# Latents, rotation and beta masks moved, delta level products without warming repeats, last MLA scores and values between output products: a four-layer fp32 transformer on one core

## The reference

```python
a_mat = beta[..., :, None] * jnp.einsum('nhcid,nhcjd->nhcij', k, k) * d_strict
sol = lax.linalg.triangular_solve(a_mat, rhs, left_side=True, lower=True, unit_diagonal=True)
```

## Time and profile before

| what | us |
|---|---|
| median of 3 runs | 1282.39 (1282.03 to 1291.31) |
| the profiled execution | 1290.47 |
| its span in the trace | 1288.3 |
| TensorE busy | 1237.2 |
| VectorE busy | 734.5 |
| ScalarE busy | 352.6 |

### The profile page before, as it was taken

The page is one execution under the profiler, slowest core; times in us unless marked ns, Lnnn a source line. Parts: engine busy times, 40 slices in busy tenths (PEclk is TensorE's granted clock), DMA queues, the critical chain, the costliest instruction groups (busy, mean ns, idle before and its releaser), DMA issues. The chain is left out here.

```text
span 1288.3 us, 18514 instructions
## 1 busy us (share of the span) xinstructions
PE 1237.2 (96%) x7285; PEld 885.2 (69%) x7285; DVE 734.5 (57%) x1467; ACT 352.6 (27%) x756; POOL 46.0 (4%) x92
## 2 busy tenths in 40 slices
PE   7999999999999999999999989999899999998997
PEld 5887548996446674599944468658567587575783
DVE  3154366766443135567644448883886178856872
ACT  2253311211002134112200043242551232425422
POOL 1100000000000000000000000100200000102000
PEclk9999899999999999999999999998999999999999
DMA  9732105545543532335445453130010433210000
GB/s 278 261 133 70 66 1 197 193 137 194 171 156 130 175 109 108 128 136 195 146 181 195 139 157 130 67 131 1 1 51 1 165 130 131 83 50 1 2 2 33
DMA packets 65854, 149.25 MB, mean 116 GB/s; under 512 B 2098, under 2 KB 8136, under 8 KB 65768
## 3 DMA queue, kind: packets, MB, share of 16 engines
q1 hardware_dynamic: 62432, 141.63, 31.3%
q0 software_dynamic: 1216, 3.52, 1.0%
q10 hardware_dynamic: 2119, 2.91, 0.9%
HBM read 146.95 MB, written 1.07 MB: 115 GB/s over the span
## 5 line engine op out<-in xcount | busy, mean ns | idle before, releaser
L1368 ACT ACTIVATE region<-banks 128x384 f32<-128x384 f32 (+8 forms) x159 | 77.1, 485 | 298.4 <-PE banks L444 104.9
L444 PE MATMUL banks<-hnT,weight_slabs 128*128 128x256 f32 x576 | 126.6, 380 | 3.4 <-DVE hnT L1856 3.4
L444 PEld LDWEIGHTS banks<-hnT,weight_slabs 128*128 128x128 f32 x576 | 108.8, 190 | 20.1 <-DVE hnT L1856 4.1
L496 PE MATMUL banks<-weight_slabs,region 128*128 128x512 f32 x256 | 115.1, 592 | 0.0
L496 PEld LDWEIGHTS banks<-weight_slabs,region 128*128 128x128 f32 x256 | 48.5, 190 | 60.3 <-issue 60.3
L496 PE MATMUL banks<-region 128*128 128x512 f32 x192 | 87.6, 592 | 0.0
L1839 DVE TENSOR_TENSOR region<-weight_slabs 128x1024 f32<-128x1024 f32 x32 | 39.2, 1225 | 80.3 <-PE banks L496 76.4
L1839 DVE TENSOR_TENSOR region<-region 128x256 f32<-128x256 f32 (+23 forms) x160 | 74.2, 464 | 16.9 <-ACT region L1725 11.8
L1997 DVE TENSOR_TENSOR region<-banks,region 128x128 f32<-128x128 f32 x40 | 11.7, 292 | 120.4 <-PE banks L611 95.3
L1839 DVE TENSOR_TENSOR region<-weight_slabs,region 128x1024 f32<-128x1024 f32 x64 | 78.2, 1221 | 1.1
L496 PEld LDWEIGHTS banks<-region 128*128 128x128 f32 x192 | 36.5, 190 | 45.9 <-issue 45.9
(11 more groups left out here) (364 smaller groups left out, 2045.6 us busy)
## 6 DMA issues: line engine op xcount, KB each, us to landing
weight_slabs<-in_mlp_w SPq DMA_DIRECT2D x32, 2048.0 KB, 8.9
weight_slabs<-in_w_in SPq DMA_DIRECT2D x10, 2048.0 KB, 7.8
weight_slabs<-in_od_w_in SPq DMA_DIRECT2D x6, 2048.0 KB, 8.0
weight_slabs<-in_ev_w_in SPq DMA_DIRECT2D x4, 2048.0 KB, 10.6
weight_slabs<-in_w_out SPq DMA_DIRECT2D x4, 2048.0 KB, 8.9
weight_slabs<-in_ev_w_out SPq DMA_DIRECT2D x2, 2048.0 KB, 8.0
weight_slabs<-in_od_w_out SPq DMA_DIRECT2D x2, 2048.0 KB, 7.7
weight_slabs<-in_w_in SPq DMA_DIRECT2D x2, 2016.0 KB, 7.7
```

The costliest lines, as they stand in the source:

```text
L444: ins = mm(view(ps, b + i * S, (1, S)), view(slabs, o + k * width + c0, (1, P)), view(hnT, k * S, (1, S)), start=k == 0, stop=k == KC - 1)
L496: ins = mm(view(ps, b, (1, 512)), view(R, act + k * st, (1, P)), view(w, wt + k * step_, (1, 512)), start=n == 0 and k == 0, stop=n == 7 a ...
L1368: say(A(dst, view(ps, b, *(dims or ((1, n),)), np_=np_), ACT.Copy, scale=scale), read("scalar", *key))
```

## The change

- TensorE: the `cT` transposes move into the RWKV inverse, behind its last Z products (hook "X"). Decay groups 2 and 3 come behind the `Yr` products of the second chunk instead of ahead of them.
- Seven of the eight warming products of the delta inverse go; the one ahead of base row 0 stays. Scores, probability transposes, values and gate steps get other places; scores 5, three transposes and values 2 to 5 move behind the inverse, between U, GS, PU, the `mixR` transposes and KS. The two halves of a level follow each other without a hook between them.
- The last Z products start when the two blocks of VT that they read are masked (`cross_blocks_ready`); VectorE masks VT in eight half-width pieces, not four.
- The beta factors are multiplied into the masks once, behind the RWKV output, so the base system and `early_blocks` of levels 0 and 1 need one multiply instead of two.
- VectorE: `rope` moves ahead of base row 0, `rwkv_variance` ahead of the G evictions, the multiply that norms q and k behind the last `Yr` adds, `state_keys` behind VT, `rwkv_finish` and the maximum of scores 5 behind the U evictions of the first chunk. `intra_mask` takes half of both directions at a time. Queries are negated in their copy, so the row minimum of the negated scores replaces maximum and sign.
- ScalarE: latent copies around the first `Ur` copies, the RWKV `rstd` ahead of the MLA copies, key copies of the rotation behind the `ukv` copies, exponentials 4 and 5 behind the inverse.

```diff
                          cst[q:q + 64, C_ID + q:C_ID + q + 64], start=True, stop=True)
         close(ins, ("VT", tag, c))
+    between("Y", 2)
     pe.wait_ge(*at("early_blocks_ready", tag, 2))
     for c in range(2):
         b = open_(("Y", tag, 2, c), ring)
...
     for c in range(2):
-        pe.wait_ge(*at("bank_read_by_vector", "VT", tag, c))
+        pe.wait_ge(*at("cross_blocks_ready", tag, c))
...
             fill(2)
-        elif what not in ("Yhalf", "Zhalf"):
+        elif what == "X":
+            for t in range(T):
+                transposes(("cT", L, t), [view(R, LOW + t * 376 + 24, (1, P)), view(R, LOW + t * 376 + 152, (1, 64)),
+                                          view(R, LOW + t * 376 + 216, (1, P))], "a", [at("latents_ready", L)])
+        elif (what, n) != ("Y", 2):
...
             close(ins, ("cum", L))
-            decay_group(2)
-            decay_group(3)
         if n == 0:
...
+        if n == 1:
+            decay_group(2)
+            decay_group(3)
         if n == 0:
...
-    for t in range(T):
-        transposes(("cT", L, t), [view(R, LOW + t * 376 + 24, (1, P)), view(R, LOW + t * 376 + 152, (1, 64)),
-                                  view(R, LOW + t * 376 + 216, (1, P))], "a", [at("latents_ready", L)])
     pe.wait_ge(*at("qk_normed", L))
...
-    SCORES = {("base", 10): 0, ("base", 12): 1, ("Y", 0): 2, ("Z", 0): 3, ("Y", 1): 4, ("Z", 1): 5}
-    PROBS = {("Z", 0): 0, ("Zhalf", 0): 1, ("Y", 1): 2, ("Z", 1): 3, ("VT", 2): 4, ("Z", 2): 5}
-    VALUES = {("Yhalf", 1): 0, ("Zhalf", 1): 1, ("VT", 2): 2, ("Z", 2): 3}
-    GATES = {("base", 14): 3, ("Yhalf", 0): 2, ("Zhalf", 0): 1, ("Yhalf", 1): 1, ("Zhalf", 1): 1}
-    WARM = (("base", -1), ("base", 14), ("Z", 0), ("Y", 1), ("Z", 1), ("VT", 2), ("Z", 2), ("X", 2))
+    SCORES = {("base", 10): 0, ("base", 12): 1, ("Z", 0): 2, ("Z", 1): 3, ("X", 2): 4, ("U", 0): 5}
+    PROBS = {("Y", 1): (0, 1), ("VT", 2): (2,), ("U", 0): (3,), ("GS", 0): (4,), ("PU", 0): (5,)}
+    VALUES = {("Z", 2): (0,), ("X", 2): (1,), ("GS", 0): (2,), ("mixR", 0): (3,), ("KS", 1): (4, 5)}
+    GATES = {("base", 14): 3, ("Y", 1): 1, ("VT", 2): 1, ("Y", 2): 1, ("Z", 2): 1, ("X", 2): 1}
     def mla_between(what, n):
         if what == "base" and n >= 0:
             next(up_steps, None)
             if n >= 8:
                 next(heads, None)
+        if (what, n) == ("base", -1):
+            warm(1, "five")
+        for h in VALUES.get((what, n), ()):
+            mla_values(h)
+        for h in PROBS.get((what, n), ()):
+            mla_transpose(h)
         if (what, n) in SCORES:
             mla_scores(SCORES[what, n])
-        if (what, n) in VALUES:
-            mla_values(VALUES[what, n])
-        if (what, n) in PROBS:
-            mla_transpose(PROBS[what, n])
-        if (what, n) in WARM:
-            warm(1, "five")
         for _ in range(GATES.get((what, n), 0)):
             next(gate_steps, None)
     invert(("g", L), "g", mla_between, "five")
...
+            mla_between("KS", 1)
...
-            mla_values(4)
+            mla_between("U", 0)
...
-            mla_values(5)
-            pe.wait_ge(*at("intra_masked", L, 0))
+            mla_between("GS", 0)
         else:
             pe.wait_ge(*at("bank_read_by_scalar", "mixR", L))
             out_part(0, True, False, (6, 7))
+        pe.wait_ge(*at("intra_masked", L, n))
         for d, c in chunks:
             pe.wait_ge(*at("bank_read_by_vector", "U", L, d, n))
             b = open_(("PU", L, d, n), ring)
             for h in range(6):
-                ins = mm(view(ps, b + h * 64, (1, 64)), view(R, GPT + (d * 12 + c * 6 + h) * P, (1, P)),
+                ins = mm(view(ps, b + h * 64, (1, 64)), view(R, GPT + 1536 * (1 - n) + (c * 6 + h) * P, (1, P)),
                          view(R, GU + d * 384 + h * 64, (1, 64)), start=True, stop=True)
             close(ins, ("PU", L, d, n))
         if n == 0:
+            mla_between("PU", 0)
             transposes(("mixR", L), [view(R, MIXB + t * D + k * P, (1, P)) for k in (6, 7) for t in range(T)], "v",
                        [at("rwkv_mix_ready", L)], ring)
+            mla_between("mixR", 0)
     def mix_part(name, t, ks, ready):
         transposes((name, L, t), [view(R, MIXB + t * D + k * P, (1, P)) for k in ks], "v", [at(ready, L, t)], "unit")
...
         for c in range(2):
             copy_out(view(R, W.Yk + c * H * m, (1, H * m)), "Y", tag, n, c, n=H * m)
-        between("Z", n)
-        if n == 0:
+        if n == 1:
             act.wait_ge(*at("blocks_updated", tag, 0))
             for k, col in ((0, C_E + 1), (1, C_L + 1)):
                 ins = A(view(R, W.V64 + 32 * k, (64, W.NS), (1, 32)), view(R, W.VX, (32, W.NS), (1, 32)), ACT.Copy, scale=cc(col))
                     step(ins)
                 else:
                     say(ins, up("half_blocks_placed", tag, 0))
+        between("Z", n)
+        if n == 0:
             between("Y", 1)
...
+    def latents_T(t):
...
+    latents_T(0)
     for d in range(2):
         copy_out(view(R, RU + d * 256, (1, 256)), "Ur", ("r", L, d), 0, n=256)
+    latents_T(1)
...
+    act.wait_ge(*at("rwkv_var_ready", L))
+    rstd(RSS, 8, 1.0 / 64, 1)
+    act.sem_inc(up("rwkv_rstd_ready", L)[0], 1)
     nc.scalar.preload_act_table_set("exp_and_others")
     for t in range(T):
         for hf in range(2):
-            copy_out(view(hn, QN + t * 672 + hf * 288, (1, 288)), "uq", L, t, hf, n=288, scale=96 ** -0.5)
+            copy_out(view(hn, QN + t * 672 + hf * 288, (1, 288)), "uq", L, t, hf, n=288, scale=-(96 ** -0.5))
...
     def mla_between(what, n):
-        if (what, n) == ("Y", 0):
+        if (what, n) == ("Z", 0):
             mla_exp(0)
             mla_exp(1)
-        elif (what, n) == ("Z", 0):
             mla_exp(2)
-            copy_out(view(hn, MPT(0), (1, 512)), "mPT", L, 0)
+        if (what, n) == ("Y", 1):
+            probs_T(0)
+            probs_T(1)
+        if (what, n) == ("Z", 1):
             mla_exp(3)
-            copy_out(view(hn, MPT(1), (1, 512)), "mPT", L, 1)
-        elif (what, n) in (("Y", 1), ("Z", 1)):
-            mla_exp(4 + (what == "Z"))
-            copy_out(view(hn, MPT(2 + (what == "Z")), (1, 512)), "mPT", L, 2 + (what == "Z"))
-        elif n == 2:
-            copy_out(view(hn, MPT(4 + (what == "Z")), (1, 512)), "mPT", L, 4 + (what == "Z"))
-            if what == "VT":
-                gate_tanh(0, 1)
-                nc.scalar.preload_act_table_set("natural_log_exp_and_others")
-                act.wait_ge(*at("rwkv_var_ready", L))
-                rstd(RSS, 8, 1.0 / 64, 1)
-                act.sem_inc(up("rwkv_rstd_ready", L)[0], 1)
+        if (what, n) == ("VT", 2):
+            probs_T(2)
     invert(("g", L), "g", mla_between)
+    gate_tanh(0, 1)
+    nc.scalar.preload_act_table_set("natural_log_exp_and_others")
+    mla_exp(4)
+    probs_T(3)
+    mla_exp(5)
...
+    probs_T(4)
+    probs_T(5)
...
+    for d in range(2):
+        src = view(R, W.V16, *sys_) if d == 0 else view(R, W.V16 + 15, (16, NS), (-1, 16))
+        mask = view(rww, BETA_BASE + 192 * d, *sys_) if beta else view(cst, C_S16 + 16 * d, (0, NS), (1, 16))
+        go(V.tensor_tensor(view(R, W.A + 16 * NS * d, *sys_), src, mask, MUL))
     settle()
-    if beta:
-        for d in range(2):
-            a_ = view(R, W.A + d * 16 * NS, (16 * H, 2), (16, H), (1, 16))
-            tt(a_, a_, view(sm, GBT + d * 6, (12, 2), (1, H), (0, 16)), MUL)
     signal("base_ready", tag, 0)
     if st == "r":
         step(V.tensor_copy(view(R, W.X, (16 * NS, 2), (16, NS), (1, 16)), view(cst, C_I16, (16, 2), (0, NS), (1, 16))))
     if st == "g":
+        between("base", -1)
...
+        mask = view(cst, C_MP[n], (0, NS), (1, m))
+        if beta and n < 2:
+            mask = view((sm, R)[n], (BETA_16, BETA_32)[n], (m, NS), (1, m))
+        tt(p_, view(R, src, (m, NS), (1, m)), mask, MUL)
+        if beta and n == 2:
             tt(p_, p_, view(sm, GBP + n * 12, (1, NS), (0, m)), MUL)
...
+    def transposed_block(c, d, q):
+        half = dict(p0=q, np_=64)
+        return V.tensor_tensor(view(R, W.XT + (d * NS + c * H) * P + q, (P, H), (1, 64), **half),
+                               view(ps, bank(("VT", tag, c)), (64, H), (1, 64), **half),
+                               view(cst, C_TRI + d * P + q, (0, H), (1, 64), **half), MUL)
     for c in range(2):
-        b = full(dve, "VT", tag, c)
-        for q in (0, 64):
-            half = dict(p0=q, np_=64)
-            ins = V.tensor_tensor(view(R, W.XT + c * H * P + q, (NS * P, 2), (P, H), (1, 64), **half),
-                                  view(ps, b, (0, 2), (64, H), (1, 64), **half),
-                                  view(cst, C_TRI + q, (P, 2), (0, H), (1, 64), **half), MUL)
-            if q == 0:
-                go(ins)
-            else:
-                settle()
-                say(ins, read("vector", "VT", tag, c))
+        full(dve, "VT", tag, c)
+        go(transposed_block(c, 1, 0))
```

(58 more changed lines are left out.)

37 lines of the change are left out of this document (16 added, 21 removed).

## The result

The changed kernel took 1279.83 us (median of 14 runs, 1274.97 to 1284.11). The kernel before, run beside it, took 1290.03 (14 runs, 1282.03 to 1293.11); its first three, with 1282.39 in the middle, had been low for it. The ratio is 0.9938, 95% interval 0.9921 to 0.9954: 0.6%, or 8 us, faster (the two medians lie 10.2 us apart). That is within the 1% that I called no change; the forecast was 13.7 us and "faster by over 1%" likeliest.

The account below looks back on a forecast made before the run. TensorE, busy 96% of the span, was taken as the bound. Gains of 1.2 + 0.85 + 5.6 = 7.65 us per layer, 15.3 for both, less 1.6 for the clock, gave 13.7: 1268.7 us from 1282.39, range 1260 to 1294.

Parts of the forecast that it names:

- The front: Delta rule up to the q/k transposes: these start at 1190.05 instead of 1191.25, a gain of 1.2 us per layer.
- Variance: Five VectorE instructions (3.1 us) ahead of the G evictions: TensorE waits some 0.8 us at the first `uq`.
- Rotation: Moved into VectorE's wait for the first base product: costs some 0.4 us there in place of 2.55.
- Key copies: Two ScalarE copies behind the fourth `ukv` product's copies: end at 1189.95, so q/k transposes start at 1190.05.
- The latents: Six `cT` transposes, under 0.7 us, hidden in TensorE's 1.46 us wait at the rwkv inverse's end; G can start 1.54 earlier.
- Up to level 0: From the q/k transposes to Y: 9.15 us instead of 10.0, 0.85 gained per layer, some 0.9 idle ahead of Y.
- The levels: From level 0's Y to the MLA mix transposes: 47.6 us instead of 53.2, 5.6 gained per layer.
- plain removal: Taking out the seven warming products alone would give 3.7 us of their 6.9 per layer.
- The clock: TensorE falls to 1.2 GHz once, in one of the two layers, in the level stages: 1.6 us lost.
- Rival C: Short clock falls in both layers lose 7 to 8 us of the 15.3: 1275 us; chance 0.10.
- The base: Median of runs, 1282.39 us, lies 8.1 below the profiled execution, so the forecast was put at 1268.7 instead of 1276.8.

Follow-up runs that it names:

- e7: Changed kernel with the rwkv variance again inside level 0 on VectorE and ScalarE's root of it behind the levels; 1291.7 us, ratio 1.0031 to before.
- e15: Changed kernel with two warming products added, one behind base row 14 and one behind the decays' running sums; 1278.2 us, ratio 0.9911 to before.
- e16: Changed kernel with warming products behind base row 14 and behind the running sums, and the rotation behind base row 2; 1274.5 us, ratio 0.9881 to before.
- e17: Changed kernel with warming products behind base row 14 and the running sums, and ScalarE's key copies ahead of the k/v evictions; 1279.3 us, ratio 0.9929 to before.
- e9: Changed kernel with one of the seven warming products back, behind base row 14 ahead of level 0; 1276.7 us, ratio 0.9923 to before.
- e4: Kernel before with only the seven warming products per layer left out, all else in the old order; 1305.5 us, ratio 1.0130 to before.
- e14: Kernel before with six of the seven warming products left out, the one behind base row 14 kept; 1304.9 us, ratio 1.0112 to before.
- e1: Changed kernel with the rotation's VectorE instructions behind base row 2 instead of ahead of base row 0; 1282.9 us, ratio 0.9965 to before.
- e2: Changed kernel with decay groups 2 and 3 again ahead of the second set of Yr products; 1284.2 us, ratio 0.9951 to before.
- e8: Changed kernel with the latents' six transposes again behind the last decay products, evictions behind the decay exponentials; 1281.5 us, ratio 0.9966 to before.
- e12: Changed kernel with one wide warming product added behind the running sums of the decays; 1284.6 us, ratio 0.9972 to before.
- e11: Changed kernel with the variance back inside level 0 and warming products behind base row 14 and at level 0's Z; 1290.5 us, ratio 1.0017 to before.
- e18: Changed kernel with warming products behind base row 14 and the sums, rotation behind base row 2, key copies ahead of k/v evictions; 1277.4 us, ratio 0.9908.
- e10: Changed kernel with two of the seven warming products back, behind base row 14 and at level 0's Z; 1279.7 us, ratio 0.9934 to before.

## Why the prediction was wrong, point by point

*The front: the step that failed first.* I gave it 1.2 us per layer. From U to Y, which also holds the 0.85 us ahead of level 0, the two executions differ by 0.1 us in L = 2 and nothing in L = 3: so the front lost 0.8 us. From G to the q/k transposes L = 3 is 3.7 us longer, and the rows add up: 0.5 more up to the up-projection and 1.0 more up to base row 0, both behind the variance; 0.8 for the key copies; 2.28 instead of 2.44 for the rotation; the rest, 1.6, is 3.4 us at half clock.
- *Variance.* I had it "ahead of the G evictions ... VectorE gains nothing from the earlier G". The wait at `uq` is 1.48, not 0.8, and VectorE's masks, GpSimd's picks and base row 0 inherit the delay (a wait of 1.31), which I had not followed. e7 shows that it is the variance.
- *Rotation.* "It costs some 0.4 there in place of 2.55." It took 4.9 us, because I took its durations from a place where GpSimd was idle for most of it. Yet the place itself is nearly neutral (e15, e16): the error was to count on some 2 us from it.
- *Key copies.* I counted them (up to 1189.95), but behind a fourth `ukv` product that the rotation was to bring forward; without that their place is a plain loss of 0.8 (e17: 1.55 against 0.76).

*The latents.* Hidden, as said, and more: the wait went from 1.46 to 0.80 and the clock did not fall within 15 us behind it in either layer. I had counted nothing for that. In L = 2 it fell later instead, in the second Yr products, and the 24 decay products took 4.29 us; TensorE timeline of after:

```profile
867.53 1.97 PE L1054 MATMUL banks<-region 128*128 128x64 f32 x16 [0.80 <-ACT region L1612]
869.34 1.56 PE L981 MATMUL banks<-consts,hn 128*128 128x128 f32 x12
...
893.43 1.81 PE L981 MATMUL banks<-consts,hn 128*128 128x128 f32 x7
```

*Up to level 0.* 9.15 us forecast, 9.16 and 9.15 measured, 0.80 idle.

*The levels.* 47.6 forecast at full clock. The true figure is 45.9 (e9, with one product hidden), 7.3 below before: only 0.14 us of new wait came ahead of level 1's Y, where I had left 0.4, and 1.4 us more came than the products and waits taken out; part of it is that 48 records in one run take 1.57 us where two runs of 24 took 0.88 each. The step that failed is the premise beside it, that plain removal would give 3.7 us: in the old order it costs 5 to 6.4 us of levels per layer (e4, e14). At full clock, too, it gave less than I had counted. From level 0's Y to level 1's Y e4 takes 12.03 us (947.75 - 935.72), before 11.68 with two warming products in it, for which I had 0.98 + 0.2 us: the wait for VectorE that stands at its end, 1.94 us, took both.

*The clock, the term that decided.* "I take one fall in one of the layers, 1.6 us." In the ten layers of after, e1, e2, e8 and e12, which all have the change's levels, every one fell, and they average 50.0 us instead of 45.9: 4.1 us per layer, five times the 0.8 that I took. I had the place right (Y, scores, Z and transposes of level 0) and let "gate products of 512 columns still follow" excuse it. Rival C, short falls in both layers, 7 to 8 us of 15.3 lost, is what happened; I gave it 0.10. With the front's loss of 0.8 for my gain of 1.2, part of it the clock too, the sum is -0.8 + 0.85 + 7.3 - 4.1 = 3.3 us per layer, near the 4 that the ratio shows.

*The base.* I took 8.1 us off for the median of three runs. Of 14 it lies at the profiled time, so this was the spread of the runs, not a distance.

The Trainium skill (TensorE: Matmul & The Clock Gate, "A second HAM failure mode: psum-queue depth-cycling") has short idle times between groups as the cause of a swinging clock. The traces agree in e4, e11 and e14, behind waits of 1.7 to 2.7 us. They do not bear it out for the levels of after: TensorE was not idle there, and the clock fell 2 to 4 us behind a single wait of 0.80. In e15, e17 and e18, where the product fills that wait, it fell in four layers with no wait in the 12 us before.

## What to carry to other kernels

A warming product is priced by the wait that it stands in: before taking one out, ask how long TensorE idles there without it, and leave those that stand in a wait anyway, since they cost nothing (here one of seven was worth 3 to 6 us by the medians, the 3 within the spread). When small products are put back to back, count the clock as a term of its own with several samples of it, because two executions of one kernel differ by as much as the edit is worth. Before you call a change of order neutral, look for the wait that the moved work fills (e2). And take the duration of a moved VectorE instruction from a place with the same neighbours.

## What the hardware showed that I had not expected

The program up to layer L = 2's rwkv inverse is the same in all these kernels, and yet U of L = 2 began anywhere from 865.3 us (e10) to 879.8 (e12). The first 100 us of both (length, busy of the engines, granted clock):

```profile
0.00:100.00 100.00, 87.75 (x520) 75.85 (x521) 35.32 (x123) 32.21 (x88) 9.71 (x20) 0.98 0.67 218
```

```profile
0.00:100.00 100.00, 85.23 (x447) 73.98 (x448) 28.90 (x102) 26.36 (x70) 9.71 (x20) 0.88 0.61 196
```

All of the 14.5 us arises in the first 200 us or so: TensorE's 1000th record starts at 205.7 and 220.3, its 4000th at 793.2 and 807.7. In e12 that part holds 31 us at half clock, in e10 7.

How long the clock stayed low in the levels went with how far behind the first Y product it fell: 3.4 us in the four layers where that was 3.57 us or more, 17.1 in seven of the eight from 2.8 to 3.53, 6.8 in four of the six below. So falls a tenth of a microsecond apart ended over 6 us apart. I can't say why; no run was made for it.

VectorE's instructions with both inputs in SBUF grew beside GpSimd's picks (0.38 to 0.93 us, 0.53 to 0.81), while those that read a bank and have one input in SBUF did not (0.53 in both). The Trainium skill (SBUF — State Buffer, "Who interferes with whom") says just that of two SBUF inputs against a GpSimd instruction that reads SBUF. It accounts for the rotation's place too. Ahead of base row 0 it takes 4.9 us, of which 1.97 are time that VectorE otherwise waits there, so 2.9 are left; behind row 2 it takes 2.4, and the three adds that then stand beside the picks grow by 0.8 together (e1), so 3.2. Whatever such work stands beside the picks pays.
